# A two-block transformer kernel on one Trainium2 core: query projections in three passes with low halves from GpSimd, one-hots by digits, and 28 instead of 24 expert projections beside the spreading

## The reference

```python
def peer_ffn(x, w_query, sub_keys, expert_down, expert_up):
    ...
        q = (xc @ w_query).reshape(C, PEER_HEADS, 2, PEER_HALF)
        sc = jnp.einsum('thpd,hpnd->thpn', q, sub_keys).astype(jnp.float32)
        top_s, top_i = lax.top_k(sc, PEER_TOPK)
        cand_s = (top_s[:, :, 0, :, None] + top_s[:, :, 1, None, :]).reshape(C, PEER_HEADS, PEER_TOPK * PEER_TOPK)
        cand_i = (top_i[:, :, 0, :, None] * PEER_NKEYS + top_i[:, :, 1, None, :]).reshape(C, PEER_HEADS, PEER_TOPK * PEER_TOPK)
        best_s, best_pos = lax.top_k(cand_s, PEER_TOPK)
        experts = jnp.take_along_axis(cand_i, best_pos, axis=-1)
        gates = jax.nn.softmax(best_s, axis=-1)
        ...
        act = jax.nn.gelu(jnp.einsum('cd,chkd->chk', xc, u).astype(jnp.float32), approximate=False)
        w = (gates * act).astype(xc.dtype)
        return jnp.einsum('chk,chkd->cd', w, vv)
```

## Time and profile before

| what | us |
|---|---|
| median of three runs | 1725.54 (1721.66 to 1726.55) |
| the profiled execution, its own time | 1728.26 |
| its span in the profile | 1726.2 |
| TensorE busy in the span | 1564.6 |
| VectorE busy | 1074.9 |
| ScalarE busy | 699.1 |
| GpSimd busy | 5.8 |
| mean granted TensorE clock | 0.955 |

### The profile page before, as it was taken

The page is one execution under the profiler, slowest core; times in us unless marked ns, Lnnn a source line. Parts: engine busy times, 40 slices in busy tenths (PEclk is TensorE's granted clock), DMA queues, the critical chain, the costliest instruction groups (busy, mean ns, idle before and its releaser), DMA issues. The chain is left out here.

```text
span 1726.2 us, 28966 instructions
## 1 busy us (share of the span) xinstructions
PE 1564.6 (91%) x8809; PEld 1383.0 (80%) x8809; DVE 1074.9 (62%) x2752; ACT 699.1 (40%) x1526; POOL 5.8 (0%) x13
## 2 busy tenths in 40 slices
PE   2997789998998999999999999879999997869987
PEld 1664578887997888999999999779999997658885
DVE  3577457957997776666666666555555554266663
ACT  0343211113323443544444444346555554336552
POOL 0000000000000000000000000000000000000000
PEclk9998789999999999999999999989999999679997
DMA  6410043442224555555555555374444441075410
GB/s 246 164 38 1 2 160 111 153 153 75 92 90 142 194 191 188 194 184 182 194 184 182 194 184 183 127 261 135 151 152 137 134 139 45 1 250 165 121 26 25
DMA packets 162586, 239.33 MB, mean 139 GB/s; under 512 B 41808, under 2 KB 91472, under 8 KB 161488
## 3 DMA queue, kind: packets, MB, share of 16 engines
q1 hardware_dynamic: 162160, 238.34, 42.2%
q10 hardware_dynamic: 352, 0.07, 0.0%
HBM read 237.09 MB, written 1.28 MB: 138 GB/s over the span
## 5 line engine op out<-in xcount | busy, mean ns | idle before, releaser
L187 PE MATMUL experts_acc<-experts_uh,experts_wh 128*128 128x512 f32 x512 | 201.5, 394 | 5.7 <-DVE experts_ul L1579 5.7
L188 PE MATMUL experts_acc<-experts_ul,experts_wh 128*128 128x512 f32 x512 | 201.1, 393 | 0.0
L189 PE MATMUL experts_acc<-experts_uh,experts_wl 128*128 128x512 f32 x512 | 200.1, 391 | 0.0
L1132 PE MATMUL plain_u<-ffn_h,down_raw 128*128 128x256 f32 x832 | 192.1, 382 | 0.4 <-PEq L1217 0.4
L1552 ACT ACTIVATE experts_uh<-ffn_h 128x512 fp32r<-128x512 f32 x256 | 147.1, 624 | 83.7 <-PE experts_acc L189 79.1
L189 PE MATMUL projection<-hT_high,down_low 128*128 128x256 f32 x608 | 172.1, 283 | 0.0
L188 PE MATMUL projection<-hT_low,down_high 128*128 128x256 f32 x608 | 172.0, 283 | 0.0
L187 PE MATMUL projection<-hT_high,down_high 128*128 128x256 f32 x608 | 171.7, 282 | 0.0
L1132 PEld LDWEIGHTS plain_u<-ffn_h,down_raw 128*128 128x128 f32 x832 | 154.1, 192 | 19.5 <-issue 1.1
L1579 DVE TENSOR_TENSOR experts_ul<-ffn_h,experts_uh 128x512 fp32r<-128x512 f32 x256 | 164.7, 684 | 3.0 <-ACT experts_uh L1552 3.0
L187 PE MATMUL mix_a_pj<-mix_a_wh,hT_high 128*128 128x384 f32 x384 | 136.8, 356 | 17.0 <-DVE mix_a_wl L560 17.0
(11 more groups left out here) (274 smaller groups left out, 3014.9 us busy)
## 6 DMA issues: line engine op xcount, KB each, us to landing
down_raw<-in_downT SPq DMA_DIRECT2D x256, 256.0 KB, 3.4
ffn_h<-in_up SPq DMA_DIRECT2D x256, 256.0 KB, 2.8
mix_a_w_raw<-in_wa SPq DMA_DIRECT2D x48, 768.0 KB, 5.9
block_w_raw<-in_w SPq DMA_DIRECT2D x16, 768.0 KB, 6.6
mix_b_w_raw<-in_wb SPq DMA_DIRECT2D x16, 768.0 KB, 6.7
route_raw<-in_route SPq DMA_DIRECT2D x16, 576.0 KB, 3.7
wo<-in_wo SPq DMA_DIRECT2D x2, 2048.0 KB, 10.4
mix_a_w_raw<-in_wa SPq DMA_DIRECT2D x16, 256.0 KB, 3.3
```

Of the source, the lines that this page charges most:

```text
L187: pe.matmul(out, lhs[0], rhs[0], start=start, stop=False, skip_group_check=True)
L188: pe.matmul(out, lhs[0], rhs[1], start=False, stop=False, skip_group_check=True)
L189: return pe.matmul(out, lhs[1], rhs[0], start=False, stop=stop, skip_group_check=True)
L1132: mm = pe.matmul(self.u[b][:, 0:SEQ], self.raw[b][:, k, :], self.h[:, k, :], start=k == 0, stop=k == KD - 1, skip_group_check=True)
```

## The change

Constants: `EARLY` 28 to 24 and `LATE` 24 to 28, so still 52 chunks are ready for the last block. The class `Plain` is renamed `Ahead` and carries `hT` too.

In route_phase the query projections go in three passes. ScalarE rounds the weights (`weight_high`, two halves of 128x512 each, one step ahead), GpSimd subtracts (`weight_low`), TensorE makes 24 fp32r matmuls instead of 8 plain ones.

```diff
+        @block.gpsimd
+        def _(pool):
+            def weight_low(hp, b, i):
+                for h in range(2):
+                    k = slice(KD // 2 * h, KD // 2 * (h + 1))
+                    pool.wait_ge(w_highs, hp * 2 + (h + 1))
+                    pool.tensor_tensor(w_low[b % 2][:, k], raw[b][:, k], w_high[b % 2][:, k].bitcast(F32),
+                                       ALU.subtract).then_inc(w_lows, 1)
...
-                    mm = pe.matmul(qp[b % 2][:, 0:SEQ], raw[b][:, k, :], plain.h[:, k, :], start=k == 0, stop=k == KD - 1,
-                                   skip_group_check=True)
+                    if k % (KD // 2) == 0:
+                        pe.wait_ge(w_lows, hp * 2 + (k // (KD // 2) + 1))
+                    mm = three_passes(pe, qp[b % 2][:, 0:SEQ], [v[b % 2][:, k, :] for v in (w_high, w_low)],
+                                      [v[:, k, :] for v in hT], k == 0, k == KD - 1)
...
+            def weight_high(hp, b, i):
+                act.wait_ge(landed[b], i * 16 + 16)
+                wait(act, q_ready, hp - 1)
+                for h in range(2):
+                    k = slice(KD // 2 * h, KD // 2 * (h + 1))
+                    act.activation(w_high[b % 2][:, k], raw[b][:, k], ACT.Copy).then_inc(w_highs, 1)
```

```diff
-                for q in range(Q):
-                    col = slice(g * Q + q, g * Q + q + 1)
-                    last = dve.tensor_scalar(a1[b][:, q, :], iota[:], slotT["i1"][:, col], slotT["gate"][:, col],
-                                             ALU.is_equal, ALU.mult)
-                last.then_inc(a1_ready, 1)
+                dve.tensor_tensor(a1[b][:].rearrange("p q (h l) -> p q h l", l=FINE),
+                                  coarse_of[:, q].unsqueeze(3).broadcast_to([P, Q, COARSE, FINE]),
+                                  fine_of[:, q].unsqueeze(2).broadcast_to([P, Q, COARSE, FINE]), ALU.mult).then_inc(a1_ready, 1)
...
+            def split_low(n):
+
+                b = splits(n) % 2
+                dve.wait_ge(highs, splits(n) + 1)
+                dve.tensor_tensor(low[b][:], raw[n % 3][:], high[b][:].bitcast(F32), ALU.subtract).then_inc(lows, 1)
             for g in range(GROUPS + 1):
                 if g < GROUPS:
                     onehots(g)
+                for n in split_chunks:
+                    if first_group(n) - 1 == g:
+                        split_low(n)
                 if g > 0:
                     merge(g - 1)
...
+            def split_high(n):
+
+                act.wait_ge(landed[n % 3], landed_by(n))
+                if splits(n) >= 2:
+                    act.wait_ge(ahead.projected, (EARLY + split_chunks[splits(n) - 2]) * 2 + 2)
+                act.activation(high[splits(n) % 2][:], raw[n % 3][:], ACT.Copy).then_inc(highs, 1)
...
+                for n in split_chunks:
+                    if first_group(n) - 2 == g:
+                        split_high(n)
```

More of the change, by code:

```diff
@@ L1208, in over_chunks, with route_phase @@
             one(i * 2 + b, b)
-def route_phase(nc, weights, hT, sbt, slots, raw, landed, early, plain):
+def route_phase(nc, weights, hT, sbt, slots, raw, landed, early, ahead):
     HP = 2 * HEADS_P
@@ L1267, in steps, with _ @@
                 one((rounds - 1) * NW + b, b, rounds - 1)
+        @block.sync
+        def _(sp):
+            with sp.Fori(0, HP // NW - 1) as i:
+                for b in range(NW):
+                    sp.wait_ge(s_ready, i * NW + b + 1)
+                    sp.dma_start(raw[b][:], weights[i * NW + b + NW]).then_inc(landed[b], 16)
+            over_chunks(sp, 2, EARLY + 2, lambda n, b: ahead.load(sp, n, b))
+        @block.gpsimd
[6 more added lines that the diff above has]
+                                       ALU.subtract).then_inc(w_lows, 1)
+            steps(pool, weight_low)
         @block.tensor
@@ L1289, in _ @@
             scores_of(HP - 1, NW - 1)
-            over_chunks(pe, 0, EARLY, lambda n, b: plain.project(pe, n, b))
-            for n, src in enumerate((index[0], index[1], gate)):
+            over_chunks(pe, 0, EARLY, lambda n, b: ahead.project(pe, n, b))
+            for n, src in enumerate((index[1], coarse, fine, gate)):
                 pe.wait_ge(cols_ready, n + 1)
@@ L1301, in one, with early_chunk @@
                 act.activation(qh[b % 2][:], qp[b % 2][:, 0:SEQ], ACT.Copy).then_inc(q_kept, 1)
+            weight_high(0, 0, 0)
             steps(act, one)
-            over_chunks(act, 0, EARLY, lambda n, b: plain.gelu(act, n, b, early[:, n, :]))
+            def early_chunk(n, b):
+                ahead.gelu(act, n, b, early[:, n, :])
+            over_chunks(act, 0, BEFORE_GATE, early_chunk)
             act.wait_ge(shifted_ready, 1)
             act.activation(gate[:], shifted[:], ACT.Exp).then_inc(gate_exp, 1)
+            over_chunks(act, BEFORE_GATE, EARLY, early_chunk)
         @block.vector
@@ L1377, in _, with spread_phase @@
             last.then_inc(cols_ready, 1)
-def spread_phase(nc, slots, iota, early, spread, plain):
+def spread_phase(nc, slots, iota, early, spread, ahead):
     Q = 4
@@ L1387, in spread_phase, with steps_by @@
     BANKS = 4
-    joins = [min(((n + 1) * KD * GROUPS + STEPS - 1) // STEPS + 1, GROUPS) for n in range(LATE)]
+    COARSE = P // FINE
+    BATCH = 8
+    def steps_by(g):
+        return LEAD + (STEPS - LEAD) * (g + 1) // GROUPS if g >= 0 else 0
+    joins = [min(next(g for g in range(GROUPS) if steps_by(g) >= (n + 1) * KD) + 2, GROUPS) for n in range(LATE)]
     def merged_rows(g):
@@ L1405, in spread_phase, with first_group, is_split, splits @@
         block = c.enter_context(nc.Block())
+        def first_group(n):
+            return next(g for g in range(GROUPS) if steps_by(g) > n * KD)
+        def is_split(n):
+            return n >= 2 and n % 3 != 0
+        def splits(n):
+            return sum(is_split(m) for m in range(n))
+        split_chunks = [n for n in range(LATE) if is_split(n)]
+        def landed_by(n):
+            return sum(m % 3 == n % 3 for m in range(2, n + 1)) * 16
         @block.sync
         def _(sp):
-            for n in range(EARLY + 2, READY):
-                plain.load(sp, n, n % 2)
+            for n in range(2, LATE):
+                if n >= 3:
+                    if is_split(n - 3):
+                        sp.wait_ge(lows, splits(n - 3) + 1)
+                    else:
+                        sp.wait_ge(ahead.projected, (EARLY + n - 3) * 2 + 2)
+                sp.dma_start(raw[n % 3][:], ahead.down[EARLY + n]).then_inc(landed[n % 3], 16)
@@ L1473, in gelu @@
                     one = act.activation(early[:, c, t:], u[:, t:SEQ], ACT.Gelu)
-                one.then_inc(plain.done, 1)
+                one.then_inc(ahead.done, 1)
+            def split_high(n):
[3 more added lines that the diff above has]
+                act.activation(high[splits(n) % 2][:], raw[n % 3][:], ACT.Copy).then_inc(highs, 1)
             for g in range(GROUPS):
```

117 lines of the change are left out of this document (80 added, 37 removed).

## The result

| | before | after |
|---|---|---|
| median, same chip, us | 1719.76 (1715.45 to 1726.55, 6 runs) | 1731.88 (1728.35 to 1732.46, 6 runs) |
| the profiled execution's own time | 1728.26 | 1732.46 |
| its span | 1726.2 | 1730.7 |

After takes 1.0075 times as long, interval [1.0058, 1.0093]: 12.1 us more by the medians, some 12.9 by the ratio. The forecast was 1735 and +9.8.

What follows compares the result with a forecast made beforehand. TensorE was taken to bound spread_phase, VectorE just short of it, and the query steps. An earlier start of spread_phase (-24.4 us) and its longer duration (+34.2) gave +9.8, so 1735 us against the 1725.5 median; range 1708 to 1748.

Steps and rivals of the forecast that it cites:

- Query steps: In route_phase, three-pass projections shorten a query step from 3.90 to 3.32 us, -9.3 us over 16 steps.
- Step and head together: In route_phase, -9.3 us from faster query steps and +2.1 us for a later first query, sum -7.2 us.
- The rival in which GpSimd bounds the step: In the query steps, GpSimd's subtraction takes 2.05 us, steps 4.1 us, total 1748; GpSimd too slow or late: chance 0.09.
- Early chunks and end of the block: In route_phase, four early chunks fewer save 13.8 us and the shorter end of the block 3.4 us.
- the cover of 1.3 us: End of route_phase: VectorE finishes the gate at 365.6, before TensorE finishes its chunks at 366.9, so it is just covered.
- The exponential: End of route_phase: with the gate's exponential behind gelu 16, 1.5 us is left instead of 4.9, -3.4 us.
- TensorE's work in the stage: In spread_phase, TensorE's own work sums to 145.9 us against 145.7 before, if nobody waits.
- The order of the work: In spread_phase, late rounding and digit work ahead of one-hots make TensorE wait 34 us; stage 180 us, +34.2.
- The digit turns: In spread_phase, turns where VectorE makes digits, 1.9 us ahead of the one-hot pair, cost TensorE 0.6 to 1.4 us.
- VectorE keeps up: Rival in spread_phase: a rounded chunk lies ready, waits for the high halves fall away, total 1701 us; chance 0.17.
- Half: Rival in spread_phase: TensorE's lag gives ScalarE more lead, waits are 17 us instead of 34, total 1718; chance 0.13.
- The clock falls in the waits: Rival in spread_phase: TensorE's waits of 1 to 3 us could lower its clock; little counted, no separate chance given.

Runs made afterwards that it cites:

- e4: Kernel before with only the query projections in three passes, low halves on GpSimd; 1714.96 us (one run).
- e3: Kernel before with only the gate's exponential moved behind the 16th gelu instead of the 28th; 1716.62 us (one run).
- e1: Changed kernel with ScalarE rounding a chunk three groups before the one in which it starts, instead of two; median 1709.31 us, 0.9935 of before.
- e5: Changed kernel with VectorE's merge of the group before placed ahead of the low-half subtraction; 1727.71 us (one run), spreading stage 174.6 us.
- e7: e6 with the spreading stage's low-half subtractions on GpSimd instead of VectorE; median 1733.33 us, 1.0092 of before.
- e6: e1 with the digits' one-hots made for 4 groups at a time instead of 8; median 1716.11 us, 0.9987 of before.

## Why the prediction was right, point by point

**Query steps: right.** Two steps of after on TensorE are 3.29 us apart, forecast 3.32:

```profile
237.32 0.61 PE L1302 MATMUL route_sp<-route_raw,route_qh 128*128 128x128 f32 x4
...
240.61 0.61 PE L1302 MATMUL route_sp<-route_raw,route_qh 128*128 128x128 f32 x4
```

GpSimd's subtraction, in ns as minimum, median and maximum, was put at 1.35 us from VectorE's 0.683 and the memset:

```profile
L1281 POOL TENSOR_TENSOR route_w_low<-route_raw,route_w_high x32: 1267/1287/1302, 227.5 to 279.9; 128x512 fp32r<-128x512 f32 x32
```

It is 1.88 times VectorE's time. The ratio from the Trainium skill (GPSIMD Engine Reference, "Performance versus the Vector engine"), 1.96, is close. The first subtraction of after starts at 227.48, 0.7 us after ScalarE's first rounding (226.77), and is not longer than the others, so the load of some 6 us by its section "Architecture" did not appear. Step and head together were forecast at -7.2; e4 gives -6.9. The rival in which GpSimd bounds the step falls.

**Early chunks and end of the block: right.** VectorE's slot copy was forecast at 368.5 and stands at 369.17, with the block's start 0.5 us later than before:

```profile
365.90 0.49 DVE L1413 TENSOR_TENSOR route_gate<-route_gate,route_ginv 128x128 f32<-128x128 f32 x2
369.17 0.42 DVE L1523 COPY spread_i<-slots 128x256 f32<-128x256 f32 x1 [2.77 <-PEq L1221]
```

VectorE is done with the gate at 366.39 and TensorE with its chunks at about 367.8; the cover of 1.3 us that I gave VectorE is 1.4. The exponential was worth 3.4 in the sum and 3.7 in e3. Corrected for the start the block is 24.2 us shorter, forecast 24.4. What the prediction did not name is the clock: staying at the upper level is worth about 2 us to the spreading stage (e3). It was in the sum unseen, since 145.9 was built from full-speed rows while before's 145.7 holds a slow start.

**TensorE's work in the stage: right.** The first group's matmuls come 4.97 us after the start (forecast 4.9), the last 176.7 us after it (forecast 177):

```profile
374.14 1.05 PE L1571 MATMUL spread_g<-spread_a 128*128 128x128 f32 x8
```

```profile
545.83 1.05 PE L1571 MATMUL spread_g<-spread_a 128*128 128x128 f32 x8
...
548.76 0.81 SPq L1632 DMA_DIRECT2D ffn_h<-in_up  x2
```

**The order of the work: right, in size and cause.** Forecast 34 us of waits of TensorE, and 25 us of VectorE before `spread_low` at 1.5 to 2 each; measured 33.7 over the sum, and 26.5 in 16 (1.66 each). The turns carried by hand up to group 33 can be set beside the trace. Behind the first group TensorE's weight loads wait there in twelve places too (the two waits of a split taken together): 0.9, 1.3, 1.4, 0.5, 1.3, 3.1, 1.3, 0.9, 1.6, 1.2, 1.5 and 1.5, where the prediction has 0.9, 1.6, 1.5, 0.7, 1.6, 3.2, 1.5, 1.2, 1.8, 1.2, 1.9 and 1.4. That is 16.4 against 18.5, in the same order and within 0.5 us in every place, so the size of the total is not luck. e1 removes the late rounding and 21.5 us go; e5 halves the wait and 5.0 go. The digit turns were put at 0.6 to 1.4 us each; in e1, where they stand alone, they are 0.74 to 1.44. Two details were wrong. VectorE's work was put at 11 us more, some 143; it is busy 136.6 us against 131.3 before, 5.3 more, which changes nothing since its sum does not set the stage. And I looked for all of TensorE's loss, some 30 us, in the wait for the one-hots. TensorE makes the first steps of a split chunk ahead of that group's matmuls, so it already waits there for the low half, and the waits stand in two places, 15.5 + 2.7 at the one-hots and 9.5 at L191. The prediction let that first wait out and still had the sum, because TensorE's waits at the two places share one delay.

**Rivals.** "VectorE keeps up" did not occur, but its condition was the right one: e1 makes it true and gives 1709, not 1701, because digit turns and small waits stay (12.2 us over the work, of which PEld shows 7.1 at the digits). "Half" falls with the 33.7 us. "The clock falls in the waits" came true once, which the mean of 0.99 over the stage hides. In group 16 a split and a turn with digits meet, TensorE stands still for 2.40 us, and soon after it the clock is at its lower level, from 419.2 to 422.6. First three rows of the timeline, then two windows (last field but two: clock):

```profile
417.71 1.13 PE L1571 MATMUL spread_g<-spread_a 128*128 128x128 f32 x8 [2.40 <-DVE spread_a L1503]
...
420.18 1.91 PE L1571 MATMUL spread_g<-spread_a 128*128 128x128 f32 x8
...
421.74 0.56 PE L191 MATMUL plain_u<-hT_high,spread_high 128*128 128x256 f32 x1
```

```profile
415.00:418.00 3.00, 0.60 (x5) 0.42 (x4) 2.85 (x8) 0.00 (x0) 0.00 (x0) 1.00 0.51 175
420.00:422.00 2.00, 2.00 (x11) 2.00 (x11) 0.95 (x2) 0.00 (x0) 0.00 (x0) 0.50 0.00 0
```

The four matmuls of the next group take 1.56 us (420.18 to 421.74) instead of 0.89, and with the passes on both sides of them TensorE loses about 1.5 us. The prediction counted little for this, and it is small; but 31.8 us of waits and 1.5 of the clock are what makes up the 33.7, so that these lie so near to 34 is in that part luck.

**The total.** +9.8 forecast, +12.1 to +12.9 measured. In the profiles the last block's first transfer is 10.2 us later (548.76 against 538.52), of which 0.5 is the later start and 9.7 the changed blocks (-24.2 and +33.9), so the forecast missed none of their terms by over a microsecond. The profiled spans differ by only 4.5 us, because the block `mix_a`, which the change leaves alone, took 400.2 us in before's profile and 393.7 in after's. The granted clock near its end goes with it. Before, then after, the 40 us that begin some 340 us behind the block's first transfer:

```profile
1459.00:1499.00 40.00, 27.16 (x105) 21.84 (x106) 11.13 (x27) 12.26 (x24) 0.00 (x0) 0.57 0.00 1
```

```profile
1469.00:1509.00 40.00, 27.46 (x131) 22.04 (x132) 13.23 (x30) 14.72 (x26) 0.00 (x0) 0.77 0.00 1
```

Over all ten profiles that block took between 393.4 and 400.2. The two or three microseconds between +9.7 and the medians are within that scatter; nothing in these runs ties them to the change, and they stay unexplained.

## What to carry to other kernels

Where engines run a written list, a wait also holds back all that stands behind it: order the work so that its input is ready a turn earlier (one number in one line was worth 22.6 us here, nearly twice the loss of the whole change). Before you call added work hidden in a stage where two engines are above 90% with two buffers between them, carry the distances from turn to turn by hand; sums of work don't show it. Before moving elementwise work to GpSimd, look at what VectorE does beside it: beside one-input searches it was free, beside products of two SBUF tensors it cost more than it saved.

## What the runs showed of the hardware that I had not expected

- **GpSimd and VectorE shut each other out.** In e7 a VectorE product of two SBUF tensors that starts during a GpSimd subtraction ends only after it: 2.65 us instead of 0.68, 2559 ns instead of 426. All 18 VectorE products of two SBUF tensors that start during one of the 17 subtractions end 0.03 to 0.65 us behind it. In the query steps, where VectorE runs searches over one tensor each, there is no such effect: 291 against 290 ns. The Trainium skill (GPSIMD Engine Reference, "Key points") says that the two share their SBUF interfaces, with contention for VectorE instructions with two SBUF inputs; the runs agree, and show that the whole instruction is held. The merge at 404.91, one of whose two inputs lies in PSUM, runs beside the subtraction in its usual 0.27.
- **GpSimd waits for VectorE in the same way.** The 128x1024 subtraction in e7 takes 2.67 to 2.84 us in the ten cases where a VectorE product of two SBUF tensors had begun 0.09 to 0.21 us before it, and 2.35 to 2.39 in the seven where none was running or at most 0.2 us of one was left. The 128x512 one in after, beside the searches, takes 1267 to 1302 ns.
- **The lower clock differs from run to run in identical code.** In the stretch near the end of `mix_a` shown above, the mean clock is 0.57 or 0.58 in the profiles of before, e5, e6 and e7, and the block takes 398.8 to 400.2 us; in the other six it is 0.69 to 0.79, and the block takes 393.4 to 395.8. The 6.5 us between before and after are half of what this change costs.
